# Sum stores and resident operand loads on other queues, and a bank read ahead of a tile's sums

## The chip, the cores and the metric

The kernel runs on one core of a Trainium2 chip. The metric is the device time of one execution in microseconds (us), as the median of several runs. The engines are TensorE (PE in the profile), VectorE (DVE), ScalarE (ACT), GpSimd (POOL) and SyncE (SP), which only issues transfers here. Each engine works through its own list of instructions in the written order, and they meet by semaphores.

## The reference

One layer of a decoder trunk on x of 2048 positions by 1024 features, all float32. The layer is a spatial-gating mixer, then a dense perceptron of four times the width with a squared ReLU, each behind an RMS norm and added to x, and a final RMS norm:

```python
def reference(x, ...):
    h = rmsnorm(x, norm_mix_g[0])
    x = x + mixer_chunked_sgu(h, a_w_in[0], a_v_g[0], a_w_s[0], a_b_s[0], a_w_out[0])
    x = x + channel_mlp(rmsnorm(x, norm_mlp_g[0]), mlp_w1[0], mlp_w2[0])
    return rmsnorm(x, final_g)

def channel_mlp(h, w1, w2):
    a = jax.nn.relu(h @ w1)
    return (a * a) @ w2
```

The mixer computes z = gelu(h @ w_in), splits it into u and v, mixes normed v within chunks of 128 positions by a causal matrix for each of 8 groups, and returns (u * s) @ w_out.

## The kernel before, in words

**Precision.** Every float32 operand is split into an upper part (a copy in fp32r, written by ScalarE, `_hi`) and a lower part (raw minus upper, written by VectorE, `_lo`). A product is three passes on TensorE: hi times hi, hi times lo, lo times hi (`PASSES`).

**Stages.** The mixer runs in 4 blocks of 512 positions (`block_pe`, `block_act`, `block_dve`). After the last block come 168 steps, numbered g. The perceptron is computed with a scheme of seven products of half-sized matrices in place of eight (`STEPS = 7`). Seven steps are a cycle. The up projection has 16 cycles u (`UP`), steps 0 to 111 (`SECOND` = 112), of 24 matmuls of 512 columns each; the down projection has 8 cycles, steps 112 to 167, of 48 matmuls each. Step 0 starts at 609.03 us, step 7 at 653.6 us, step 17 at 713.87 us, step 56 at 930.67 us and step 112 at about 1245 us of the span.

**Up projection.** For positions 0 to 1023 (cycles 0 to 7, the first pair) the seven operands `x_raw[0..6]` of 1024 KB stay resident; the second pair's replace them one by one around step 56. They come from the DRAM tensor `xs` (`up_operand`, line 319): those with `op < S2` are halves of the normed, transposed x1 (`x1T`), the others are sums of such, made by GpSimd. A weight `u_raw[g % 4]` of 512 KB is loaded for each step (`up_weight`, line 301), asked for when step g - 4 is done. ScalarE (`ahead`, `split_u`) and VectorE split the weight of step g + 2 at their step g, and then read the banks of step g: ScalarE those of steps 0, 2, 3 and 6 of a cycle (`keep_bank`, line 681), VectorE those of 1, 4 and 5 (`add_bank`, line 892). TensorE's step needs the split weight, the split operand, and that its banks have been read; the banks of step 3 of a cycle are those of step 1.

**Sums.** For each of two tiles j, ScalarE squares two of the four results into `sums[j][:, 0:2]` (`finish_first`, line 685, at step 6 of a cycle), and VectorE computes the rest with six instructions (`finish_second`, line 896), tile 0 at step 0 of the next cycle and tile 1 at its step 1, ahead of the bank read of that step. SyncE stores `sums[j]`, 1792 KB, to `a2s` (`keep_sums`, line 335) at steps 1 and 2 of the next cycle. ScalarE waits for the stores (`a2_stored`, line 689) before it writes the next cycle's; VectorE comes behind ScalarE by `first_half`.

**GpSimd's jobs.** `add_up` (line 438): load 1 MB to `job`, four instructions, store 1 MB; 40 in all, one buffer, so a job starts when the store before has landed. They make the sums of weights (`w1sum`, `w2sum`) and operands (`xs[:, 4:8]`). Twenty are done in the mixer; the loop at line 500 does two in each of cycles 0 and 1, one in each later cycle, and none in cycles 6 to 8. The first four of that loop are the second pair's operand sums; they wait until ScalarE's last `x1T` store has landed (line 453).

**Queues.** SyncE's list (line 350 on) issues in this order: the weights of the mixer; at the end of the last block operands 0 and 1 and the first four weights; behind the mixer's last product the operands 2 to 5; then the store of x1 to `x1s` (2 MB), and from step 0 on, at the end of each step, the next weight, operand 6 at step 1, the second pair's operands at steps 49 to 55, the sum stores, and for the down projection `down_operand` and `down_weight`. ScalarE's list has at the end of the last block the splits of operands 0 and 1 and of two weights, and then the squares of the four x1 tiles (line 642).

Of the kernel before, what the change touches and what calls it, by code (L numbers as in the profile page):

```python
# [30 lines left out]
def build(nc: bass.Bass, x, norm_mix_g, norm_mlp_g, final_g, a_w_in, a_v_g, a_w_s, a_b_s, a_w_out,  # L31
# [122 lines left out]
    with ExitStack() as ctx:  # L154
# [45 lines left out]
        a2_stored = [sem(f"a2_stored{s}") for s in range(2)]  # L200
# [77 lines left out]

        block = ctx.enter_context(nc.Block())

        @block.sync
        def _(sp):
# [36 lines left out]
            def up_operand(b, i):  # L319
                op = ACT_OPERAND[i]  # L320
                if op < S2:
                    sp.wait_ge(x1T_stored, 16 * 4 * (b + 1))
                else:
                    sp.wait_ge(job_stored, sums_stored("x", b))
                sp.dma_start(x_raw[i][:, :, :], xs[b][:, op, :].rearrange("p (k f) -> p k f", f=N))\
                    .then_inc(x_loaded[i], 16)

            def down_operand(d):
                n, i = d // STEPS, d % STEPS
                for s in range(2):  # L330
                    sp.wait_ge(a2_stored[s], 16 * 2 * (n + 1))
                sp.dma_start(a_raw[d % SLOTS][:, :, :], a2s[n][:, i, :].rearrange("p (k f) -> p k f", f=N))\
                    .then_inc(a_loaded[d % SLOTS], 16)

            def keep_sums(u, j):

                sp.wait_ge(second_half, 6 * (2 * u + j + 1))
                sp.wait_ge(first_half, 4 * (2 * u + j + 1))
                to = a2s[u // 2].rearrange("p i (k f) -> p i k f", f=N)[:, :, 2 * (u % 2) + j, :]
                sp.dma_start(to, sums[j][:, :, :]).then_inc(a2_stored[j], 16)  # L340
# [9 lines left out]
            for q in range(BLOCKS):  # L350
# [10 lines left out]
                else:  # L361

                    sp.wait_ge(mix_done, BLOCKS * G)
                    up_operand(0, 0)
# [3 lines left out]
                    up_operand(0, 1)  # L368
# [3 lines left out]
                    sp.wait_ge(products, done(number(q, 11)))  # L372
                    for i in range(2, 6):
                        up_operand(0, i)
                sp.wait_ge(x1_attn, (q + 1) * 2 * TT)
                sp.dma_start(x1s[q], x1[:, :, :]).then_inc(x1_stored, 16)
                if q < BLOCKS - 1:
                    sp.wait_ge(x1_stored, 16 * (q + 1))
                    sp.wait_ge(x1n_ready, (q + 1) * TT)
                    sp.dma_start(x1[:, :, :], x_v[q + 1]).then_inc(x1_loaded, 16)  # L380
            second = UP // PAIRS * STEPS
            for g in range(SECOND):
# [3 lines left out]
                if g == 1:  # L386
                    sp.wait_ge(x1_stored, 16 * BLOCKS)
                    sp.wait_ge(x1n_ready, BLOCKS * TT)
                    up_operand(0, 6)
                if second - STEPS <= g < second:  # L390
                    up_operand(1, g % STEPS)
                if g >= STEPS and g % STEPS in (1, 2):
                    keep_sums(g // STEPS - 1, g % STEPS - 1)
# [9 lines left out]
            for j in range(2):  # L403
                keep_sums(UP - 1, j)
            for d in range(SLOTS, DOWN * STEPS):
# [3 lines left out]
                if d == STEPS:  # L409
                    for h in range(2):  # L410
                        sp.wait_ge(a2_stored[h], 16 * UP)
# [8 lines left out]
        def _(pool):  # L420
# [78 lines left out]

            for u in range(UP):  # L500
                pool.wait_ge(products, step_done(u * STEPS))
                if not UP // PAIRS - 2 <= u <= UP // PAIRS:
                    next_jobs(2 if u < 2 else 1)
# [21 lines left out]
        def _(act):  # L525
# [74 lines left out]
            def block_act(q, last):  # L600
# [36 lines left out]
                else:  # L637
# [3 lines left out]
                    split_x(0, 1)  # L641
                for t in range(TT):
                    act.wait_ge(x1_attn, q * 2 * TT + TT + t + 1)
                    square(x1[:, t, :], x1_sq, t, x1_squares(q) + t)

# [39 lines left out]
            def finish_first(u, j):  # L685

                m = 2 * u + j
                if u:
                    act.wait_ge(a2_stored[j], 16 * u)
# [17 lines left out]
            for g in range(LAST):  # L707
                c, i = (g if g < SECOND else g - SECOND) // STEPS, g % STEPS
                ahead(g)
# [32 lines left out]
        def _(dve):  # L742
# [153 lines left out]
            def finish_second(u, j):  # L896
# [3 lines left out]
                a21 = r21[:, j, :]  # L900
                dve.wait_ge(act_read, banks_read(g + 6, j))
# [21 lines left out]
            for g in range(SECOND):  # L923
                c, i = g // STEPS, g % STEPS
                ahead(g)
                if c and i < 2:
                    finish_second(c - 1, i)
                if i in (1, 4, 5):
                    to = {1: c11, 4: c22, 5: c12}[i]
                    for j in range(2):  # L930
                        dve.wait_ge(act_read, banks_read({1: g - 1, 4: g - 1, 5: g - 3}[i], j))
                        add_bank(g, j, to[:, j, :])
                renew(g)
# [214 lines left out]
```

## Time and profile before

| | before |
|---|---|
| median of 3 runs | 1867.68 us (1865.74 to 1870.53) |
| profiled execution | 1867.12 us |
| its span | 1865.4 us |
| PE busy | 1827.3 us (98%) |
| DVE busy | 1052.2 us (56%) |
| ACT busy | 777.3 us (42%) |
| POOL busy | 401.2 us (22%) |
| DMA moved | 437.02 MB, 234 GB/s in the mean |
| SyncE's queue | 333.99 MB |
| GpSimd's queue | 92.80 MB |
| ScalarE's queue | 8.93 MB |
| granted TensorE clock | 0.993 |

Busy times are of the profiled execution, in us of its span. A row of waits names the engine and line that waited, what ended the wait, and the total, count and longest. A timeline row starts with start and duration; brackets show the idle time before it and its releaser.

### The profile page before, as it was taken

What the parts mean: (1) busy time and instruction counts of PE and PEld (TensorE: products, weight loads), DVE (VectorE), ACT (ScalarE), POOL (GpSimd) and SP (SyncE); (2) the same over time, 40 slices, a digit from 0 to 9 for tenths busy, and PEclk for the clock granted to TensorE, in tenths of its full rate; (3) what the DMA queues carried; (4) which work ended last, traced back from release to release, by engine and by line L of the source; (5) the groups of instructions that cost most, each with busy time, mean ns of one, the idle gap of its engine ahead of it and who ended that gap; (6) DMA issues with size and microseconds to landing.
All of it is one profiled execution on the core that took longest, in us unless ns stands there. A gap on an engine that the chain in (4) does not pass through costs nothing.

```text
span 1865.4 us, 20258 instructions
## 1 busy us (share of the span) xinstructions
PE 1827.3 (98%) x8329; PEld 1519.8 (81%) x8329; DVE 1052.2 (56%) x1009; ACT 777.3 (42%) x866; POOL 401.2 (22%) x390
## 2 busy tenths in 40 slices
PE   7999999999999998999989999999999999999998
PEld 6888888888888787888778888888888888888886
DVE  4464365265246656645565555557567666866665
ACT  5533544443442733344464433445333335333332
POOL 3341450351341033320001221110134202000001
PEclk9999999999999999999999999999999999999999
DMA  8545754762854787875856776699976754854552
GB/s 299 208 170 182 256 213 143 286 229 92 311 198 144 274 265 263 277 282 206 284 201 227 263 273 246 220 338 355 330 267 255 273 188 181 294 201 181 190 209 98
DMA packets 132092, 437.02 MB, mean 234 GB/s; under 512 B 7304, under 2 KB 8352, under 8 KB 117152
## 3 DMA queue, kind: packets, MB, share of 16 engines
q1 hardware_dynamic: 105488, 333.99, 50.4%
q0 software_dynamic: 25168, 92.80, 14.0%
q10 hardware_dynamic: 1344, 8.93, 1.2%
q8 instruction: 66, 1.08, 0.2%
q14 instruction: 26, 0.21, 0.0%
HBM read 309.87 MB, written 125.83 MB: 234 GB/s over the span
## 4 chain that ended last, share of the span: by engine, by line
PE 91%; DMA 3%; DVE 3%; ACT 1%; issue 1%; SPq 0%; POOL 0%; POOLq 0%; DVEq 0%; ACTq 0%
PE bank L1116 60%; PE bank L977 28%; PE bank L1014 2%; DMA u_raw<-in_mlp_w 1%; PE bank L1001 1%; DMA a_raw<-a2s 1%; DMA w_raw<-in_a_w_in 0%; DVE sums L912 0%; DVE u_lo L752 0%; DVE Y L919 0%; DVE r L902 0%; DVE sums L910 0%; DVE sums L908 0%; DVE sums L905 0%; ACT r L683 0%
## 5 line engine op out<-in xcount | busy, mean ns | idle before, releaser
L1116 PE MATMUL bank<-x_hi,u_hi 128*128 128x512 f32 x896 | 351.8, 393 | 16.1 <-DVE c L894 11.5
L1116 PE MATMUL bank<-x_lo,u_hi 128*128 128x512 f32 x896 | 350.7, 391 | 0.0
L1116 PE MATMUL bank<-x_hi,u_lo 128*128 128x512 f32 x896 | 350.6, 391 | 0.0
L1116 PE MATMUL bank<-d_hi,a_hi 128*128 128x512 f32 x896 | 348.8, 389 | 1.4 <-issue 1.0
L1116 PE MATMUL bank<-d_lo,a_hi 128*128 128x512 f32 x896 | 348.6, 389 | 0.0
L1116 PE MATMUL bank<-d_hi,a_lo 128*128 128x512 f32 x896 | 348.6, 389 | 0.0
L752 DVE TENSOR_TENSOR u_lo<-u_raw,u_hi 128x1024 fp32r<-128x1024 f32 x112 | 145.5, 1301 | 225.4 <-ACT u_hi L533 225.4
L894 DVE TENSOR_TENSOR Y<-bank,Y 128x512 f32<-128x512 f32 x208 | 137.8, 686 | 175.9 <-PE bank L1116 175.8
L746 DVE TENSOR_TENSOR w_lo<-w_raw,w_hi 128x2048 fp32r<-128x2048 f32 x48 | 119.4, 2494 | 187.5 <-ACT w_hi L528 187.5
L538 ACT ACTIVATE d_hi<-d_raw 128x2048 fp32r<-128x2048 f32 x56 | 107.4, 1919 | 279.8 <-DMA d_raw<-w2sum 150.9
L1116 PEld LDWEIGHTS bank<-x_hi,u_hi 128*128 128x128 f32 x896 | 169.6, 189 | 54.0 <-issue 15.7
L1116 PEld LDWEIGHTS bank<-x_hi,u_lo 128*128 128x128 f32 x896 | 169.5, 189 | 35.5
L1116 PEld LDWEIGHTS bank<-d_hi,a_hi 128*128 128x128 f32 x896 | 168.2, 188 | 37.1 <-issue 1.3
L1116 PEld LDWEIGHTS bank<-x_lo,u_hi 128*128 128x128 f32 x896 | 169.6, 189 | 35.1
L1116 PEld LDWEIGHTS bank<-d_lo,a_hi 128*128 128x128 f32 x896 | 168.2, 188 | 34.9
L1116 PEld LDWEIGHTS bank<-d_hi,a_lo 128*128 128x128 f32 x896 | 168.2, 188 | 34.9
L533 ACT ACTIVATE u_hi<-u_raw 128x1024 fp32r<-128x1024 f32 x112 | 118.4, 1057 | 171.5 <-DMA u_raw<-in_mlp_w 109.7
L769 DVE TENSOR_TENSOR a_lo<-a_raw,a_hi 128x2048 fp32r<-128x2048 f32 x56 | 132.4, 2364 | 20.2 <-ACT a_hi L547 20.1
L758 DVE TENSOR_TENSOR d_lo<-d_raw,d_hi 128x2048 fp32r<-128x2048 f32 x56 | 128.7, 2298 | 19.5 <-ACT d_hi L538 19.5
L547 ACT ACTIVATE a_hi<-a_raw 128x2048 fp32r<-128x2048 f32 x56 | 107.4, 1918 | 65.7 <-DMA a_raw<-a2s 65.7
L683 ACT ACTIVATE c<-bank 128x512 f32<-128x512 f32 x96 | 56.9, 597 | 164.8 <-PE bank L1116 164.7
L528 ACT ACTIVATE w_hi<-w_raw 128x2048 fp32r<-128x2048 f32 x48 | 91.5, 1913 | 33.6 <-DMA w_raw<-in_a_w_in 25.5
(107 smaller groups left out, 2739.6 us busy)
## 6 DMA issues: line engine op xcount, KB each, us to landing
a2s<-sums SPq DMA_DIRECT2D x32, 1792.0 KB, 10.7
a_raw<-a2s SPq DMA_DIRECT2D x56, 1024.0 KB, 7.5
w_raw<-in_a_w_in SPq DMA_DIRECT2D x32, 1024.0 KB, 5.9
job<-in_mlp_w POOLq DMA_DIRECT2D x32, 1024.0 KB, 7.0
u_raw<-w1sum SPq DMA_DIRECT2D x64, 512.0 KB, 4.4
d_raw<-w2sum SPq DMA_DIRECT2D x32, 1024.0 KB, 4.9
u_raw<-in_mlp_w SPq DMA_DIRECT2D x48, 512.0 KB, 5.5
d_raw<-in_mlp_w SPq DMA_DIRECT2D x24, 1024.0 KB, 5.2
```

The lines of the kernel that those rows point to most:

```text
L528: act.activation(w_hi[w % SLOTS][:, :, :], w_raw[w % SLOTS][:, :, :], ACT.Copy)\
L533: act.activation(u_hi[g % SLOTS][:, :, :], u_raw[g % SLOTS][:, :, :], ACT.Copy)\
L538: act.activation(d_hi[d % SLOTS][:, :, :], d_raw[d % SLOTS][:, :, :], ACT.Copy)\
L547: act.activation(a_hi[d % SLOTS][:, :, :], a_raw[d % SLOTS][:, :, :], ACT.Copy)\
L683: act.activation(to, bank_of(g, j)[:, :], func).then_inc(act_read, 1)
L746: dve.tensor_tensor(w_lo[s][:, :, :], w_raw[s][:, :, :], f32(w_hi[s][:, :, :]), ALU.subtract)\
L752: dve.tensor_tensor(u_lo[s][:, :, :], u_raw[s][:, :, :], f32(u_hi[s][:, :, :]), ALU.subtract)\
L758: dve.tensor_tensor(d_lo[s][:, :, :], d_raw[s][:, :, :], f32(d_hi[s][:, :, :]), ALU.subtract)\
L769: dve.tensor_tensor(a_lo[s][:, :, :], a_raw[s][:, :, :], f32(a_hi[s][:, :, :]), ALU.subtract)\
L894: dve.tensor_tensor(rows, bank_of(g, j)[:, :], rows, ALU.add).then_inc(dve_read, 1)
L977: ins = pe.matmul(BANK[s][j][:, :], stationary(x_part, k, j), moving(y_part, k, j), start=first and k == 0 and n == 0, stop=final and k == ...
L1116: ins = pe.matmul(bank_of(g, j)[:, :], stationary[x_part][:, k, j * P:(j + 1) * P], moving[y_part][:, k, :], start=i in (0, 1, 3) and k == ...
```

## The change

Three things move. The stores of the sums go from SyncE to GpSimd, each in two parts: operands 0 and 1 ahead of a cycle's first job, with a semaphore `a2_first`, and operands 2 to 6 behind it, with `a2_second`. ScalarE waits for the first part of the cycle before, and VectorE has a wait of its own for the second (`finish_second`). The loads of operands 2 to 5 of the first pair, of all seven of the second pair, and the last store of x1 go from SyncE to ScalarE. And at step 1 of a cycle VectorE reads its two banks ahead of tile 1's sums. The request for operand 6 of the first pair stands one step later.

```diff
@@ up_operand, now for a given engine @@
+        def up_operand(engine, b, i):
+            op = ACT_OPERAND[i]
+            if op < S2:
+                engine.wait_ge(x1T_stored, 16 * 4 * (b + 1))
+            else:
+                engine.wait_ge(job_stored, sums_stored("x", b))
+            engine.dma_start(x_raw[i][:, :, :], xs[b][:, op, :].rearrange("p (k f) -> p k f", f=N))\
+                .then_inc(x_loaded[i], 16)
@@ SyncE @@
             def down_operand(d):
                 n, i = d // STEPS, d % STEPS
                 for s in range(2):
-                    sp.wait_ge(a2_stored[s], 16 * 2 * (n + 1))
+                    sp.wait_ge(a2_first[s], 16 * 2 * (n + 1))
+                    sp.wait_ge(a2_second[s], 16 * 2 * (n + 1))
-            def keep_sums(u, j):
-
-                sp.wait_ge(second_half, 6 * (2 * u + j + 1))
-                sp.wait_ge(first_half, 4 * (2 * u + j + 1))
-                to = a2s[u // 2].rearrange("p i (k f) -> p i k f", f=N)[:, :, 2 * (u % 2) + j, :]
-                sp.dma_start(to, sums[j][:, :, :]).then_inc(a2_stored[j], 16)
-                    sp.wait_ge(products, done(number(q, 11)))
-                    for i in range(2, 6):
-                        up_operand(0, i)
-                sp.wait_ge(x1_attn, (q + 1) * 2 * TT)
-                sp.dma_start(x1s[q], x1[:, :, :]).then_inc(x1_stored, 16)
                 if q < BLOCKS - 1:
+                    sp.wait_ge(x1_attn, (q + 1) * 2 * TT)
+                    sp.dma_start(x1s[q], x1[:, :, :]).then_inc(x1_stored, 16)
-                if g == 1:
+                if g == 2:
                     sp.wait_ge(x1_stored, 16 * BLOCKS)
                     sp.wait_ge(x1n_ready, BLOCKS * TT)
-                    up_operand(0, 6)
-                if second - STEPS <= g < second:
-                    up_operand(1, g % STEPS)
-                if g >= STEPS and g % STEPS in (1, 2):
-                    keep_sums(g // STEPS - 1, g % STEPS - 1)
+                    up_operand(sp, 0, 6)
-            for j in range(2):
-                keep_sums(UP - 1, j)
@@ GpSimd @@
+            def keep_sums(u, part):
+
+                ops, count, of, kept = ((slice(0, 2), 4, first_half, a2_first),
+                                        (slice(2, STEPS), 6, second_half, a2_second))[part]
+                for j in range(2):
+                    pool.wait_ge(of, count * (2 * u + j + 1))
+                    to = a2s[u // 2].rearrange("p i (k f) -> p i k f", f=N)[:, ops, 2 * (u % 2) + j, :]
+                    pool.dma_start(to, sums[j][:, ops, :]).then_inc(kept[j], 16)
+
             for u in range(UP):
                 pool.wait_ge(products, step_done(u * STEPS))
-                if not UP // PAIRS - 2 <= u <= UP // PAIRS:
-                    next_jobs(2 if u < 2 else 1)
+                if u:
+                    keep_sums(u - 1, 0)
+                paused = UP // PAIRS - 2 <= u <= UP // PAIRS
+                if not paused:
+                    next_jobs(1)
+                if u:
+                    keep_sums(u - 1, 1)
+                if u < 2:
+                    next_jobs(1)
+            for part in range(2):
+                keep_sums(UP - 1, part)
@@ ScalarE, end of the last block @@
                     split_x(0, 1)
+                    act.wait_ge(products, done(number(q, 11)))
+                    up_operand(act, 0, 2)
+                    up_operand(act, 0, 3)
                 for t in range(TT):
                     act.wait_ge(x1_attn, q * 2 * TT + TT + t + 1)
                     square(x1[:, t, :], x1_sq, t, x1_squares(q) + t)
+                if last:
+                    act.dma_start(x1s[q], x1[:, :, :]).then_inc(x1_stored, 16)
+                    up_operand(act, 0, 4)
+                    up_operand(act, 0, 5)
@@ ScalarE, finish_first and the loop over steps @@
                 if u:
-                    act.wait_ge(a2_stored[j], 16 * u)
+                    act.wait_ge(a2_first[j], 16 * u)
+                if second - STEPS <= g - 1 < second:
+
+                    act.wait_ge(products, step_done(g - 1))
+                    up_operand(act, 1, (g - 1) % STEPS)
                 ahead(g)
@@ VectorE, finish_second and the loop over steps @@
+                if u:
+                    dve.wait_ge(a2_second[j], 16 * u)
                 dve.wait_ge(act_read, banks_read(g + 6, j))
-                if c and i < 2:
-                    finish_second(c - 1, i)
+                if c and i == 0:
+                    finish_second(c - 1, 0)
                 if i in (1, 4, 5):
                     to = {1: c11, 4: c22, 5: c12}[i]
                     for j in range(2):
                         dve.wait_ge(act_read, banks_read({1: g - 1, 4: g - 1, 5: g - 3}[i], j))
                         add_bank(g, j, to[:, j, :])
+                if c and i == 1:
+                    finish_second(c - 1, 1)
```

## Rows read from the trace of the kernel before

**Rows 1.** TensorE's waits: waiting line, what ended it; total us, count, longest.

```profile
PE bank L1116 <- DVE c L894: 11.5, 3, 6.0
PE bank L1116 <- issue: 3.6, 2, 2.6
PE bank L1116 <- DVE d_lo L758: 0.5, 1, 0.5
```

**Rows 2.** Timeline of TensorE: start, us, instruction, [idle before, releaser].

```profile
635.24 0.47 PE L1116 MATMUL bank<-x_hi,u_hi 128*128 128x512 f32 x1 [2.65 <-issue]
...
713.87 0.77 PE L1116 MATMUL bank<-x_hi,u_hi 128*128 128x512 f32 x1 [5.20 <-DVE c L894]
...
930.67 0.69 PE L1116 MATMUL bank<-x_hi,u_hi 128*128 128x512 f32 x1 [1.86 <-DVE u_lo L752]
...
955.31 0.76 PE L1116 MATMUL bank<-x_hi,u_hi 128*128 128x512 f32 x1 [6.02 <-DVE c L894]
```

**Rows 3.** Chain of waits in order of time: start, us, what.

```profile
635.24 5.73 PE bank L1116 x24
...
675.94 13.71 DMA u_raw<-in_mlp_w
...
713.87 204.08 PE bank L1116 x888
...
955.31 268.17 PE bank L1116 x1176
...
1268.74 582.37 PE bank L1116 x2568
```

**Rows 4.** Stretch 705 to 720: length, busy PE PEld DVE ACT POOL, clock, DMA, GB/s.

```profile
705.00:720.00 15.00, 9.80 (x33) 7.57 (x32) 11.51 (x12) 2.72 (x4) 5.68 (x5) 0.77 0.94 327
```

**Rows 5.** Timeline of SyncE's queue, issues with their time.

```profile
609.06 1.96 SPq L325 DMA_DIRECT2D x_raw<-xs  x4
...
664.94 0.60 SPq L340 DMA_DIRECT2D a2s<-sums  x1
```

**Rows 6.** Timeline of ScalarE around the first steps; the next instruction is at 639.24.

```profile
607.75 1.06 ACT L566 ACTIVATE junk<-x 128x1024 bf16<-128x1024 f32 x1 [21.23 <-DVE x L813]
...
615.00 1.91 ACT L543 ACTIVATE x_hi<-x_raw 128x2048 fp32r<-128x2048 f32 x1
...
638.87 0.33 ACTq L597 DMA_DIRECT2D xs<-x1T  x1
```

**Rows 7.** Timeline of VectorE: an operand's lower half, bank reads, a tile's sums.

```profile
616.94 2.29 DVE L763 TENSOR_TENSOR x_lo<-x_raw,x_hi 128x2048 fp32r<-128x2048 f32 x1 [2.10 <-ACT x_hi L543]
...
713.03 1.28 DVE L894 TENSOR_TENSOR c<-bank,c 128x512 f32<-128x512 f32 x2
...
740.03 1.23 DVE L752 TENSOR_TENSOR u_lo<-u_raw,u_hi 128x1024 fp32r<-128x1024 f32 x1 [5.12 <-ACT u_hi L533]
741.17 0.69 DVE L902 TENSOR_TENSOR r<-r 128x512 f32<-128x512 f32 x1
...
744.42 0.69 DVE L914 TENSOR_TENSOR sums<-sums 128x512 f32<-128x512 f32 x1
```

**Rows 8.** Timeline of GpSimd: a job's load and store, the next job's instructions and store.

```profile
649.79 0.83 POOL L454 DMA_DIRECT2D job<-xs  x1 [36.26 <-DMA xs<-x1T]
...
664.19 0.78 POOL L475 DMA_DIRECT2D xs<-job  x1 [0.30 <-POOL job L473]
...
684.41 1.29 POOL L467 TENSOR_TENSOR job<-job 128x512 f32<-128x512 f32 x1 [11.92 <-DMA job<-xs]
...
690.10 0.78 POOL L475 DMA_DIRECT2D xs<-job  x1 [0.30 <-POOL job L473]
```

**Rows 9.** 600 to 720: landings of job transfers, of sum stores; job load of 718.8.

```profile
DMA to landing us min/median/max: 5.3/7.3/12.6
...
DMA to landing us min/median/max: 8.6/12.4/17.3
...
job<-xs POOLq DMA_DIRECT2D x1, 1024.0 KB, 8.3
```

More of the change, by code:

```diff
@@ L199, in build @@
         first_half, second_half = sem("first_half"), sem("second_half")
-        a2_stored = [sem(f"a2_stored{s}") for s in range(2)]
+        a2_first = [sem(f"a2_first{s}") for s in range(2)]
+        a2_second = [sem(f"a2_second{s}") for s in range(2)]
         x1_added = [sem(f"x1_added{i}") for i in range(4)]
@@ L317, in down_weight @@
                 sp.dma_start(d_raw[d % SLOTS][:, :, :], src).then_inc(d_loaded[d % SLOTS], 16)
[L319 to L326, printed above, removed]
             def down_operand(d):
@@ L363, in _ @@
                     sp.wait_ge(mix_done, BLOCKS * G)
-                    up_operand(0, 0)
+                    up_operand(sp, 0, 0)
                     sp.wait_ge(products, done(number(q, 8)))
@@ L367, in _ @@
                     up_weight(1)
-                    up_operand(0, 1)
+                    up_operand(sp, 0, 1)
                     sp.wait_ge(products, done(number(q, 9)))
@@ L380, in _ @@
                     sp.dma_start(x1[:, :, :], x_v[q + 1]).then_inc(x1_loaded, 16)
-            second = UP // PAIRS * STEPS
             for g in range(SECOND):
@@ L410, in _ @@
                     for h in range(2):
-                        sp.wait_ge(a2_stored[h], 16 * UP)
+                        sp.wait_ge(a2_first[h], 16 * UP)
+                        sp.wait_ge(a2_second[h], 16 * UP)
                         sp.dma_start(Y[1][h][:, :, :], x1s[2 + h]).then_inc(Y_loaded[h], 16)
@@ L708, in _ @@
                 c, i = (g if g < SECOND else g - SECOND) // STEPS, g % STEPS
+                second = UP // PAIRS * STEPS
+                if second - STEPS <= g - 1 < second:
+                    act.wait_ge(products, step_done(g - 1))
+                    up_operand(act, 1, (g - 1) % STEPS)
                 ahead(g)
```

## The prediction

> **What bounds the kernel now.** I began with the busy shares of the page: TensorE is busy in 98% of the span, so the whole question is which of its few pauses go and which come. The list of waits gives them by what ended them [rows 1], the timeline of TensorE gives their place [rows 2], and the chain of waits gives the length of the stretches between them [rows 3]. Up to 609 us nothing that the change touches stands near a pause. From there to the end six pauses matter. Steps are numbered as in the loops, step g being one operand product of the multilayer perceptron. An undisturbed step of the up projection is 24 matmuls; the last long stretch, 2568 matmuls in 582.37 us [rows 3], makes that 5.44 us.
> The pauses are 2.65 us before step 4, 5.20 before step 17, 1.86 before step 56 and 6.02 before step 59 [rows 2]. The vector engine's reads of a bank stand behind 11.5 us in three pauses [rows 1]; less the two long ones that leaves 0.28 us, before step 10. The two small ones at the start of the down projection are 0.5 us and what the second "issue" wait leaves, 3.6 - 2.65 = 0.95 [rows 1]. After a pause TensorE runs slowly for a while: the stretch of 705 to 720 us was granted 0.77 of the clock [rows 4], between its levels of 1.2 and 2.4 GHz. Priced against 226.8 ns a matmul, the stretch from 713.87 lost 2.7 us and that from 955.31 lost 1.5; the three steps between 930.67 and 949.29 (955.31 less its pause) took 18.62 us where 16.33 were due, 2.3 lost; step 4 took 5.73, 0.3 lost [rows 2, 3]. Together: 2.95 (step 4) + 0.28 + 7.90 (step 17) + 4.15 (step 56) + 7.50 (step 59) + 1.45 = 24.2 us. That is the most this change can win. The profiled execution took 1867.12 us around a span of 1865.4; without the six pauses it would be 1842.9. The median of the runs is 0.56 above the profiled one.
> Why they are there: a store of the sums (1792 KB) is issued on SyncE's queue between weight loads, as at 664.94 [rows 5], and the chain shows a weight load issued at 675.94 that landed 13.71 us later [rows 3]. ScalarE and VectorE take everything in a written order, so a late weight makes all behind it late, and VectorE's 3.9 us of sums for the second tile then stand in front of its bank read.
>
> **The change part by part.**
> *Bank reads first.* At the second step of a cycle VectorE now reads the two banks before the second tile's six sums. Nothing is added. The reads took from 713.03 and TensorE went on at 713.87 [rows 2, 7]; at 3.9 us earlier, the 0.28 goes and most of 5.20 and 6.02 would, if all else stood still. What is late next is the weight split of the step after, which still comes behind the sums.
> *Sum stores to GpSimd's queue.* This takes the stores out of the way of the weight loads. Around step 56 the loads of the second pair's seven operands leave SyncE's queue too, for ScalarE's, each behind a wait for a step that ScalarE was about to wait for anyway. Walking ScalarE's list from step 50, weights landing in the median of some 5 us, I find step 56 served about 4 us ahead and step 59 about 2 us ahead; so 1.86 + 2.3 + 6.02 + 1.5 go, as does the 1.45 at the end, whose operand load was behind a sum store. Seven issues of 0.37 us (638.87 to the next ScalarE instruction [rows 6]) lie in ScalarE's idle time. Cover gone, this costs at most what stands there now.
> *The start of the up projection.* ScalarE now waits for the end of the mixer's last product, where SyncE issued at 609.06 [rows 5], then issues two loads, squares four tiles, and issues the store of x1 and two more loads. Before, the first square began at 607.75 [rows 6]. The wait and two issues (0.4 each) make the squares 2.1 us later, three issues more make 3.3. The split of operand 2 then moves from 615.00 [rows 6] to 618.3, its lower half from 616.94 [rows 7] to 620.2 and its end to 622.5. Step 2 is due at 619.9 (609.03 and two steps), so TensorE pauses 2.6 us there, 0.3 with the clock. In exchange weight 4 no longer stands behind 6 MB, and the pause before step 4 goes. Issues at SyncE's 0.49 each (1.96 for four [rows 5]) instead of 0.37 move this by 0.6; the bounds are 2.0 and 4.0, and I take 2.9. Operand 6 is asked for one step later on SyncE, but the x1 store that it waits for is what held it, and it has a whole step in hand: nothing.
> *The new place of the stores, and the new wait.* This is the costly part. GpSimd also does the "jobs" (load 1 MB, four tensor instructions, store 1 MB, the next only after that store landed). In cycles 0 and 1 it does two jobs each. The second part of the sums of cycle u-1 (five of seven operands) is issued behind the first job of cycle u, and VectorE may not write the sums of cycle u before it has landed. What waits behind VectorE is the weight split of the step after next, and behind that TensorE.
> The job that starts at 649.79 [rows 8] cannot start sooner, for it waits for the last x1T store. It stores at 664.19, which alone on the queues takes the least of the job transfers, 5.3 us [rows 9]: 669.5. The next load is given 6.3, between least and median 7.3; instructions to store 5.7 (684.41 to 690.10 [rows 8]): 681.5. Only now GpSimd comes to cycle 1. The first part of the sums is issued behind that store and lands some 9 us later, in time, as ScalarE wants it at about 690. Next job: store landed 687.8 (6.3), load 8.3 as in the row with a store beside it [rows 9], 5.7 more: 701.8. Behind it come the two second parts, 1280 KB each. The least landing of 1792 KB is 8.6 and of 1024 KB is 5.3 [rows 9], so 4.3 us per 1000 KB; the queue's 2304 KB up to the first tile make 10.8: 712.6. VectorE's sums for one tile take 3.9 (741.17 to 745.11), a split 1.15, the bank read and TensorE's start 0.8 [rows 7]: step 17 can start at 718.4. It would have been due at 713.87 - 5.20 - 0.28 - 0.3 = 708.1. **A new pause of 10.3 us** and 2.7 of slow clock.
> Cycle 2, the same way: the stores of cycle 1 end at 701.8 + 16.3 = 718.1; the fourth job's load is behind them, 722.5; its store 728.2; landed 734.5; next load 742.8; store 748.5; first tile's second part 759.3; step 24 at 765.1. It is due at 718.4 + 38.1 + 2.7 = 759.2: **a pause of 5.9** and 2.3 slow. In cycle 3 there is one job only, the stores land about 783 to 790 while VectorE comes to them at about 790: no pause. Later the second part lands some 27 us after the first step of a cycle, and VectorE comes 36 us after it.
> Bounds for the two pauses with their clock, 21.2 us: every job transfer at its least and the stores at 8.6 give about 15; 4 us more on the chain give about 25.
> The sum: 1842.9 + 2.9 + 13.0 + 8.2 = 1867.0, plus 0.56 for the median, **1867.6**: no change, because the pauses removed around 714, 931 and 955 us are paid for at steps 2, 17 and 24.
>
> **A page against it.** At 705 to 720 us the DMA engines were busy in 0.94 of the time at 327 GB/s [rows 4]. The Trainium skill (DMA: Bandwidth & Descriptors, Issuing engines are not separate DMA queues) says that transfers from whichever issuer share the same 16 engines, and that another issuer saves issue time only. By that rule the weight load at step 52 stays late and the pause before step 56 stays. The row of 13.71 us [rows 3] doesn't settle it: a full set of engines and a store ahead in the queue look alike there.
> The first VectorE sum at 741.17 runs beside no GpSimd instruction; GpSimd's issue at 649.79 took 0.83 and that at 664.19 took 0.78 with VectorE at work [rows 8]. The Trainium skill (SBUF — State Buffer, Who interferes with whom) warns that a DMA from GpSimd can be starved of descriptors by VectorE. These rows show no such thing, and the rule would put the result with the slow rival below.
>
> **The rivals.**
> (a) *Exchange*, the forecast: 1861 to 1875 by the bounds above.
> (b) *GpSimd keeps up*: VectorE's new wait never ends last. For it: GpSimd is busy in only 22% of the span. Against it: the serial chain from 649.79, each link a row. The time is 1842.9 + 2.9 + 0.56 = 1846.4; with one short pause left, 1855.
> (c) *Slower*: in cycles 1 and 2 the transfers go at the saturated ends of the rows, loads at 12.6 and sum stores at 17.3 [rows 9], since weights, jobs and sums now all run at once. Two loads (6.3 and 4.3 more) and the stores (3 to 5 more) put step 17 some 15 us later, and cycle 2 follows by 3 more: 1867.6 + 18 = 1885. The place is VectorE's wait at steps 14 and 21. It turns the result slower by over 0.3% once the two pauses pass some 22 us together, where I have 16.2.
> (d) *Queues make no difference*: shared engines keep the weights as late as they are, and the 1.86 + 2.3 at step 56 stay: 1867.6 + 4.2 = 1871.8. For it speaks the DMA share of 0.94 [rows 4]; against it, that a weight load alone needs half a megabyte in each step and gets a turn of its own.
>
> **How the numbers follow.** About 0.3%, 5.6 us, is what a measurement of this kernel can tell from no change (its three runs lie 4.8 apart). Chances: (a) 0.56, of which 0.11 under 1862, 0.39 within, 0.06 over 1873; (b) 0.26, all faster; (c) 0.14, all slower; (d) 0.04, within. So faster 0.37, same 0.43, slower 0.20. The range of 0.8 takes in (b) down to 1847 and goes up to 1878, into the lower part of (c). The forecast's own range is 1861 to 1875.
>
> **What would show it.** In the new profile: TensorE's waits by VectorE's bank reads at step 10 and 59 gone, the wait before step 4 gone and one of 2 to 4 us before step 2 (about 620 us); a VectorE gap before its first sum at about 698 to 712 us ended by a sum store, and TensorE pauses at about 708 (step 17) and 759 (step 24), 10 and 6 us; none from 800 us to the end of the up projection. If the gap on VectorE is there but ends before 702 us, (b) holds. If the weight loads around 912 us still take over 12 us to land, (d) holds. The forecast is wrong above all if GpSimd issues the second part of cycle 0 much sooner or later than 702 us.

## The result, and the profile after

The changed kernel takes 1874.1 us in the median (1873.0 to 1876.2), the kernel before, run beside it, 1869.3. The ratio of the means is 1.0031, with a 95% interval of 1.0018 to 1.0044: 5 us slower by the medians, 6 by the means. The forecast was 1867.6, no change. The profiled execution took 1874.05 us around a span of 1872.3, against 1867.12 before, so the two traces can be compared directly. Two single executions of kernels below stand far outside, at 2221.8 us (operand loads back on SyncE) and 4786.0 us (old queues); the ratios leave them out.

The page after: TensorE is still the bound, and the bytes have changed queues (rows of section 1 and 3; SyncE's queue is q1, GpSimd's q0, ScalarE's q10).

```profile
span 1872.3 us, 20356 instructions
...
PE 1827.2 (98%) x8329; PEld 1520.2 (81%) x8329; DVE 1057.5 (56%) x1009; ACT 775.1 (41%) x866; POOL 448.3 (24%) x454
...
q1 hardware_dynamic: 74576, 261.64, 38.9%
q0 software_dynamic: 40528, 151.53, 23.1%
q10 hardware_dynamic: 3072, 22.56, 3.0%
```

TensorE works as long as before, to 0.1 us. The difference is in its pauses. TensorE's timeline after, every idle time ahead of a product of the perceptron:

```profile
622.51 0.47 PE L1136 MATMUL bank<-x_hi,u_hi 128*128 128x512 f32 x1 [1.47 <-issue]
...
723.03 0.76 PE L1136 MATMUL bank<-x_hi,u_hi 128*128 128x512 f32 x1 [15.09 <-DVE c L910]
...
732.74 0.50 PE L1136 MATMUL bank<-x_hi,u_hi 128*128 128x512 f32 x1 [1.53 <-DVE u_lo L768]
...
768.79 0.47 PE L1136 MATMUL bank<-x_hi,u_hi 128*128 128x512 f32 x1 [3.12 <-DVE c L910]
...
963.27 0.47 PE L1136 MATMUL bank<-x_hi,u_hi 128*128 128x512 f32 x1 [2.16 <-DVE c L910]
...
970.97 0.50 PE L1136 MATMUL bank<-x_hi,u_hi 128*128 128x512 f32 x1 [0.40 <-DVE u_lo L768]
```

These stand before steps 2, 17, 18, 24, 59 and 60. Set against [rows 2], the pauses before steps 4 and 56 are gone, that before step 17 has grown from 5.20 to 15.09, and that before step 59 has shrunk from 6.02 to 2.16. Priced as in the prediction (5.44 us for an undisturbed step), the stretches behind the pauses took 0.3, 2.7, 0.3, 1.8 and, for the last two together, 1.9 us more than was due. The clock granted behind the pauses of steps 17, 24 and 59 was 0.68, 0.85 and 0.76 (723.1 to 731.2, 768.8 to 780 and 963.4 to 970.4 us); behind those of steps 2 and 18 it was 1.00, so the two 0.3 are not the clock's. The list is 23.8 us of pauses and 6.9 of slower work behind them, 30.7; the time without them is 1843.3, where the prediction has 1842.9. Before, the same account gave 24.2 (24.8 with two stretches of 0.3 that the prediction left out). That is 5.9 of the 6.9 us between the two executions. The rest, some 1.1, lies ahead of the first step: step 0 begins at 610.16 us and not at 609.03. In the kernels below it begins between 609.08 and 610.37, with the old queues as late as with the new; I count it to the run and not to the change.

How the long pause comes about is in the chain of waits (start, duration, what), here from 664 to 734 us:

```profile
664.74 6.25 DMA xs<-job
671.28 7.28 DMA job<-xs
...
690.97 9.80 DMA job<-xs
...
707.34 9.83 DMA a2s<-sums
...
732.74 22.07 PE bank L1136 x96
```

and in the timeline, GpSimd's rows and VectorE's:

```profile
685.96 1.43 POOL L493 DMA_DIRECT2D a2s<-sums  x2
690.97 0.75 POOL L440 DMA_DIRECT2D job<-xs  x1 [3.58 <-DMA xs<-job]
...
706.57 0.78 POOL L461 DMA_DIRECT2D xs<-job  x1 [0.30 <-POOL job L459]
707.34 1.74 POOL L493 DMA_DIRECT2D a2s<-sums  x2
...
717.19 0.69 DVE L920 TENSOR_TENSOR r<-r 128x512 f32<-128x512 f32 x1 [16.19 <-DMA a2s<-sums]
...
722.20 1.28 DVE L910 TENSOR_TENSOR c<-bank,c 128x512 f32<-128x512 f32 x2
...
725.68 1.76 DVE L926 TENSOR_TENSOR sums<-sums,r 128x512 f32<-128x512 f32 x1
```

GpSimd issues the first parts of cycle 0's sums at 685.96, behind two jobs, and the second parts at 707.34, behind a third. VectorE's first sum of cycle 1 waits 16.19 us for that store, its bank read follows at 722.20, and TensorE starts step 17 at 723.03.

### The profile page after: what moved, and what is told of

Same layout as the page of the kernel before. It is cut to its first block, busy times and chain, and to the rows that moved or that the text cites. A ratio compares the mean times of both kernels' runs of the same rounds, so it can differ in the third digit from the quotient of the medians.

```text
span 1872.3 us, 20356 instructions
## 1 busy us (share of the span) xinstructions
PE 1827.2 (98%) x8329; PEld 1520.2 (81%) x8329; DVE 1057.5 (56%) x1009; ACT 775.1 (41%) x866; POOL 448.3 (24%) x454
## 4 chain that ended last, share of the span: by engine, by line
PE 90%; DMA 4%; DVE 2%; ACT 1%; POOL 1%; issue 1%; SPq 0%; POOLq 0%; ACTq 0%; DVEq 0%
PE bank L1136 59%; PE bank L997 28%; PE bank L1034 2%; DMA job<-xs 1%; PE bank L1021 1%; DMA xs<-job 1%; DMA u_raw<-w1sum 1%; DMA u_raw<-in_mlp_w 1%; DMA a2s<-sums 1%; DMA w_raw<-in_a_w_in 0%; DVE u_lo L768 0%; ACT x_hi L547 0%; POOL job L459 0%; DVE Y L937 0%; ACT x1T L597 0%
## 5 line engine op out<-in xcount | busy, mean ns | idle before, releaser
L1136 PE MATMUL bank<-x_hi,u_hi 128*128 128x512 f32 x896 | 351.7, 392 | 23.8 <-DVE c L910 20.4
L493 POOL DMA_DIRECT2D a2s<-sums x64 | 51.2, 806 | 287.7 <-PE bank L1136 217.0
```

Source lines behind the costliest of these rows:

```text
L493: pool.dma_start(to, sums[j][:, ops, :]).then_inc(kept[j], 16)
L1136: ins = pe.matmul(bank_of(g, j)[:, :], stationary[x_part][:, k, j * P:(j + 1) * P], moving[y_part][:, k, :], start=i in (0, 1, 3) and k == ...
```

## Experiments

The theory: the pauses at steps 17, 18 and 24 come from GpSimd's list, in which the sum stores stand behind jobs that each wait for their own transfers. Cycles 0 and 1 have two jobs each, so cycles 1 and 2 begin with the list behind. The rivals: full DMA engines, or the stores' length, make VectorE wait wherever the stores are issued; or another part of the change costs the time. Unless told otherwise an edit is made to the changed kernel, and ratios are to the kernel before. All but the last two ran on one chip, the last two on another, each beside the kernel before, whose median was 1867.5 to 1868.2 us.

### The second parts ahead of the job

```diff
                 if u:
                     keep_sums(u - 1, 0)
+                    keep_sums(u - 1, 1)
                 ...
                     next_jobs(1)
-                if u:
-                    keep_sums(u - 1, 1)
```

> The changed kernel, but GpSimd issues both parts of a cycle's sum stores before the cycle's job, not around it. My theory (the serial list of GpSimd: VectorE's new wait ends late in cycles 1 and 2 only because two jobs and a job's load stand in front of the second part): the pauses before steps 17, 18 and 24 (15.09 + 1.53 + 3.12 us) and their slow clock (4.8) go, so about 1849.5 us, 1846 to 1855; pauses before steps 2 and 59 stay as they are. Rival (shared engines: the bytes of jobs, sums and weights are what takes the time, in whatever order they are issued): the second part still lands at 710 or later, step 17 still pauses 8 us or more, 1866 or more.

Measured: 1864.0 us, 0.9978 (0.9969 to 0.9987), between the two and nearer to the rival's number, 10 us under the changed kernel. No pause stands before step 17, but beside the one before step 2 there are five, of 1.2 to 5.6 us, at steps 18, 23, 25, 59 and 60. The timeline of this kernel, rows of GpSimd, ScalarE and TensorE:

```profile
685.36 3.16 POOL L493 DMA_DIRECT2D a2s<-sums  x4
690.53 0.75 POOL L440 DMA_DIRECT2D job<-xs  x1 [2.00 <-DMA xs<-job]
708.68 1.56 POOL L453 TENSOR_TENSOR job<-job 128x512 f32<-128x512 f32 x1 [17.40 <-DMA job<-xs]
...
741.99 0.63 ACT L703 ACTIVATE c<-c 128x512 f32<-128x512 f32 x1 [15.21 <-DMA a2s<-sums]
...
749.48 0.79 PE L1135 MATMUL bank<-x_hi,u_hi 128*128 128x512 f32 x1 [5.62 <-DVE u_lo L767]
```

The wait moved. The third job's load now follows 3.5 MB of sum stores in GpSimd's queue and its first instruction starts 18.15 us after its issue, where the median of the job transfers before was 7.3 [rows 9]; everything behind it in the list is later, and it is now the first part of cycle 1's sums that comes late, with ScalarE waiting 15.21 us for it. While the list is too long, the order in it decides who waits and for how long; it doesn't end the waiting. My expectation took the jobs to be free to slip; they are not.

### One job a cycle from the start

```diff
-                if u < 2:
-                    next_jobs(1)
```

> The changed kernel, but with one job instead of two in cycles 0 and 1; the three jobs fewer end up in later cycles and in the down projection. Theory (serial list): GpSimd is free at about 671 us, the second part of cycle 0 goes out at about 687 and lands before 702, so steps 17 and 24 do not pause: 1849 to 1854, less good than with the second part first only if the later jobs hold the down projection. Rival (a job's load between the two parts is enough to make the second late): step 17 still pauses over 5 us, 1862 or more.

Measured: 1867.4 us, 0.9996 (0.9988 to 1.0005). By its number this is the rival's, by its places it is not. The up projection came out as the theory says: TensorE runs without a pause from 641.85 us for 1176 matmuls, through steps 17, 18 and 24. What I had named as a proviso and given no price is the far end: the last jobs are stored later, at 1474.63 us, and SyncE's loads of the down projection, in one list, wait for the sum of weights that they make (the chain of this kernel, then TensorE's timeline):

```profile
641.85 266.59 PE bank L1134 x1176
...
1442.92 7.13 DMA job<-in_mlp_w
...
1474.63 4.57 DMA w2sum<-job
...
1479.76 8.71 DMA a_raw<-a2s
```

```profile
1493.47 0.76 PE L1134 MATMUL bank<-d_hi,a_hi 128*128 128x512 f32 x1 [12.59 <-DVE Y L908]
```

The loads behind that store cost one pause of 12.59 us. So the doubled jobs have a purpose, but not their place. That asked for a kernel that keeps all forty and moves two.

### The two doubled jobs moved to cycles 11 and 13

```diff
-                if u < 2:
+                if u in (11, 13):
                     next_jobs(1)
```

> The changed kernel with one job instead of two in cycles 0 and 1, and two instead of one in cycles 11 and 13, so that as many jobs as before are done by the down projection. With one job a cycle the up projection had pauses of 1.5, 2.1 and 2.0 us only, and the down projection one of 12.6 for a late job. Theory (serial list of GpSimd): that one goes too and a second job in a later cycle has its 38 us: 1867.4 - 12.6 - 1.25 - 2.5 of slow clock = 1851, 1848 to 1855. Rival (the second job makes its own pause in cycles 12 and 14): 1858 or more.

Measured: 1856.2 us, 0.9939 (0.9927 to 0.9950). It is 1 us outside the range of 1848 to 1855 and under the rival's 1858. Against the changed kernel's 1.0031 that is 0.0092, 17 us, from two jobs put elsewhere, and nothing stands before steps 17, 18 and 24. This settles the theory: same stores, same queues, same bytes, and the pauses go with the place of the jobs. Most of the 5 us that it lacks of the 1851 lies in one pause at the start of the down projection (the timeline of GpSimd and TensorE):

```profile
1217.19 2.79 POOL L445 TENSOR_TENSOR job<-job 128x512 f32<-128x512 f32 x1 [17.57 <-DMA job<-in_mlp_w]
...
1258.05 0.76 PE L1136 MATMUL bank<-d_hi,a_hi 128*128 128x512 f32 x1 [6.49 <-DVE a_lo L785]
```

The job of cycle 15 waits 17.57 us for its load. The second part of cycle 14's sums is issued behind it and lands at 1249.57; VectorE's sums of cycle 15 wait for that, and the splits of the down projection's operands stand behind those sums.

### The sum stores back on SyncE

```diff
@@ SyncE, each tile in one piece @@
+                if g >= STEPS and g % STEPS in (1, 2):
+                    keep_sums(g // STEPS - 1, g % STEPS - 1)
 ...
@@ GpSimd @@
-                    keep_sums(u - 1, 0)
 ...
-                    keep_sums(u - 1, 1)
@@ VectorE @@
-                if u:
-                    dve.wait_ge(a2_second[j], 16 * u)
```

with GpSimd's loop as it was before (two jobs in cycles 0 and 1). Bank reads and operand loads stay as changed.

> The changed kernel with the sum stores back on SyncE in one piece, without VectorE's wait for the second part; operand loads on ScalarE and early reads stay. Theory: no pause at steps 17 and 24; the start pauses 1.5 instead of 2.3 and 1.6 of slow clock; around steps 56 to 60 the sum stores still stand ahead of the weights, but no operand does, so about half of the 7.5 us of pauses there stay: 1853, 1850 to 1857. Rival (shared engines: whose queue the operand loads are on changes nothing): 1857 to 1859, as with the early reads alone.

Measured: 1859.7 us, 0.9958 (0.9945 to 0.9971). The 16.19 us wait of VectorE is gone and with it the long pause, which puts the loss on the stores' place a second time, from the other side. It is not as fast as I expected: it lies outside the range of 1850 to 1857 and a shade over the rival's 1857 to 1859, that is, level with the early reads alone (0.9946, below). The pause before step 56 is back. TensorE's timeline:

```profile
926.79 0.80 PE L1124 MATMUL bank<-x_hi,u_hi 128*128 128x512 f32 x1 [3.90 <-DVE u_lo L758]
```

The weight loads go with it. The longest one near step 56, here (issued between 905 and 910 us) and in the changed kernel (at 933.87), by issuer, size in KB and us to landing:

```profile
u_raw<-in_mlp_w SPq DMA_DIRECT2D x1, 512.0 KB, 19.2
...
u_raw<-in_mlp_w SPq DMA_DIRECT2D x1, 512.0 KB, 10.0
```

### The bank reads, undone and alone

Undone in the changed kernel; the second edit is its reverse, made to the kernel before:

```diff
-                if c and i == 0:
-                    finish_second(c - 1, 0)
+                if c and i < 2:
+                    finish_second(c - 1, i)
                 ...
-                if c and i == 1:
-                    finish_second(c - 1, 1)
```

> The changed kernel with VectorE's old order: at step 1 of a cycle the second tile's sums ahead of the bank reads. Theory: the early reads are worth 4 to 8 us at step 17 (the sums of the second tile took 8.1 us there beside GpSimd's instructions), about 4 at step 59, and under 4 at step 24: 1874.1 + 10 = 1884, 1879 to 1889. Rival (the reads are not what ends last, a weight or the other tile is): within 2 us of 1874.

Measured: 1883.8 us, 1.0081 (1.0065 to 1.0097), as expected, and 9.7 us over the changed kernel. TensorE's timeline:

```profile
729.85 0.77 PE L1134 MATMUL bank<-x_hi,u_hi 128*128 128x512 f32 x1 [22.41 <-DVE c L910]
...
969.97 0.76 PE L1134 MATMUL bank<-x_hi,u_hi 128*128 128x512 f32 x1 [6.03 <-DVE c L910]
```

The sums of the second tile are in front of the bank read again: step 17 pauses 22.41 us, and step 59 6.03, as in [rows 2].

> The kernel before with only VectorE's new order (bank reads ahead of the second tile's sums). Theory: the 0.28 us before step 10 goes, the 5.20 before step 17 shrinks to some 1.2 with half of its slow clock, and of the 6.02 before step 59 only 1.4 go, since the weight split of the step after is then late behind the sums: 1869.3 - 7 = 1862, 1859 to 1866. Rival (the pause only moves one step on): 1867 to 1870.

Measured: 1857.8 us, 0.9946 (0.9933 to 0.9958): 9.8 us faster than before, with all transfers where they were, and better than the 1859 to 1866 expected. No pause is left before step 17, where I had kept 1.2 us. In place of the two before steps 56 and 59 there are four, of 1.6 to 2.2 us, at steps 56, 58, 59 and 60. So this part alone is worth 10 us, in either surrounding, and the changed kernel would be faster than before had it been the only change.

### The operand loads back on SyncE

```diff
@@ SyncE @@
+                    sp.wait_ge(products, done(number(q, 11)))
+                    for i in range(2, 6):
+                        up_operand(sp, 0, i)
+                if second - STEPS <= g < second:
+                    up_operand(sp, 1, g % STEPS)
@@ ScalarE @@
-                    up_operand(act, 0, 2)
 ...
-                    up_operand(act, 1, (g - 1) % STEPS)
```

and so for the x1 store and operand 6; the sum stores stay with GpSimd.

> The changed kernel with the operand loads and the last x1 store back on SyncE; sum stores on GpSimd and early reads stay. Theory (the sum stores' new place alone makes the slowdown): the pauses of 15 and 3 us at steps 17 and 24 stay, the pause at step 2 becomes one of 2.6 before step 4, and around step 59 weights stand behind operands: 1876, 1873 to 1879. Rival (ScalarE's extra issues and waits cost something that the list of pauses hides): below 1872.

Measured: 1875.0 us, 1.0033 (1.0017 to 1.0048), level with the changed kernel. Its profiled execution was 8.6 us shorter than its median, so its pauses can't be summed to that; only their places are read: step 2's pause is gone, and the one before step 4 is back at 2.40 us. The operand loads' queue is worth nothing that can be measured.

### Around step 56

All kernels so far have pauses at steps 56 to 60, where the second pair's operands are loaded and split. In all of them ScalarE and VectorE split one operand in each of seven successive steps, 52 to 58. The edit, made to the kernel of cycles 11 and 13, in both engines' lists, spreads these splits by when each operand is needed:

```diff
                 elif second - 4 <= g < second - 4 + STEPS:
-                    split_x(1, g - second + 4)
+                    for i in {-4: (0,), -3: (1,), -2: (2, 3), 0: (4,), 2: (5,)}.get(g - second, ()):
+                        split_x(1, i)
+                elif g == second + 3:
+                    split_x(1, 6)
```

> As the one with the jobs moved later, and the second pair's operands are split at other steps, on ScalarE and VectorE: operands 2 and 3 both at step 54, 4 at 56, none at 57, 5 at 58, 6 at 59. Theory (at steps 55 to 57 ScalarE and VectorE have more to do than two steps hold, after a weight that came 10 us late): the pauses of 2.1 and 2.0 us before steps 59 and 60 and 1.9 us of slow clock go: 5 to 6 us less than that kernel, about 1846. Rival (the late weight load alone makes them, since the engines are full there): within 1.5 us of it.

Measured: 1849.7 us, 0.9908 (0.9895 to 0.9920), 6.5 us less. The up projection has no pause at all behind step 2, though the weights issued at 898 to 909 us still took 9.2 to 9.8 us to land, with all DMA engines busy (a share of 1.00 from 906 to 923 us). Part of the gain may be the 6.49 us pause at 1258, which in this kernel's profile is 1.81; the pauses at 930 to 946 were 4.5 us with no clock counted.

### The jobs off the last cycle

The edit is made to the kernel of the last section.

```diff
-                if not paused:
+                if not paused and u < UP - 1:
                     next_jobs(1)
                 ...
-                if u in (11, 13):
+                if u in (4, 10, 12):
                     next_jobs(1)
```

> As the one with the moved operand splits, but the doubled jobs are in cycles 4, 10 and 12, and cycle 15 has none, so that nothing stands between the two parts of the sum stores where the down projection's loads begin. Theory: with a job in cycle 15 its load took 15 to 18 us there, the second part landed late and TensorE paused 1.8 us (6.5 in the kernel without the moved splits) before step 113; that goes: 2 to 4 us less than 1849.7, about 1847, with a pause near 1.9 us at the start as the only one. Rival (the loads of the down projection make that pause themselves): 1849 to 1851.

Measured: 1846.5 us, 0.9881 (0.9868 to 0.9895), the fastest here: 22 us under the kernel before and 28 under the changed one. Its timeline of GpSimd and VectorE up to cycle 1, and TensorE's waits in the perceptron (line, what ended them; total, count, longest):

```profile
664.52 1.43 POOL L493 DMA_DIRECT2D a2s<-sums  x2
...
685.31 1.74 POOL L493 DMA_DIRECT2D a2s<-sums  x2
...
695.22 0.69 DVE L926 TENSOR_TENSOR r<-r 128x512 f32<-128x512 f32 x1 [1.56 <-DMA a2s<-sums]
```

```profile
PE bank L1142 <- issue: 1.5, 1, 1.5
PE bank L1142 <- DVE c L916: 1.3, 2, 1.0
```

First and second parts go out 21.4 and 22.0 us earlier than in the changed kernel, with one job less ahead of each. VectorE still waits for the store, 1.56 us in place of 16.19, and TensorE does not notice.

### The same edits with the old queues

Is the stores' move worth anything once the rest is mended? This kernel is the one before with VectorE's new order and the spread splits, all transfers as before.

> The kernel before with the early reads and the moved operand splits, all transfers where they were. Theory (the splits' place and not the queues makes the pauses before steps 59 and 60): these two, 2.2 and 2.0 us, and their slow clock go and the ones before steps 56 and 58 (1.6 and 1.7, a weight behind a sum store) stay: 1857.8 - 5 = 1853, 1851 to 1856. Rival (with the weights late behind stores, ScalarE is late anyway and the splits' order changes nothing): 1857 to 1859.

Measured: 1854.4 us, 0.9917 (0.9902 to 0.9932). The kernel with the moved transfers and placed jobs is 0.0036 below that, some 7 us, on the same chip. How the 7 us divide over stores, operand loads and jobs was not measured. What the traces do show is the stores' effect around step 56. In the four kernels with the sum stores on SyncE (before, early reads alone, stores back on SyncE, and this one) the longest weight landing there is 15.5 to 19.2 us, and TensorE pauses 1.6 to 3.9 us before step 56. In the eight with the stores on GpSimd it is 8.8 to 10.9 us, and none pauses there. So the stores out of the weights' way remove that pause; their share of the 7 us stays open.

## Why the prediction was wrong

The exchange was right as a mechanism, and so were the places of the pauses at steps 2, 17 and 24. The two after step 56 were forecast as gone, and the one at step 18 not at all. The sum was 6.6 us short of the profile (24.1 forecast, 30.7 found): step 17 +4.8, step 18 +1.8, steps 59 and 60 +4.4, less 3.3 at step 24 and 1.2 at the start. So two things failed: the links of GpSimd's chain up to step 17 were sized too short, and step 59 was put at nothing. That the time still lies inside the forecast's 1861 to 1875 is in part luck, by the two terms that erred the other way. Term by term:

**What the pauses cost before, and the floor.** 1842.9 forecast, 1843.3 found. Right. (The prediction speaks of six pauses and sums seven.)

**Start pause, step 2.** 2.9 forecast, 1.7 found (1.47 and 0.3). TensorE started at 622.51, which is the 622.5 forecast, but by two errors that cancel: step 0 began 1.1 us later than the prediction reckoned, and the way from there was 1.1 us shorter. The three issues priced as a delay lay beneath the last square (timeline of ScalarE):

```profile
614.83 1.06 ACT L570 ACTIVATE junk<-x 128x1024 bf16<-128x1024 f32 x1
614.87 0.33 ACTq L653 DMA_DIRECT2D x1s<-x  x1
```

In the six kernels below with the same start that begin step 0 at 609.1 to 609.7 us the pause is 1.5 to 2.0 us too, so the 2.6 was an overlap left out and not the mixer's doing. The pause before step 4 went, as forecast.

**Step 17.** 13.0 forecast, 17.8 found (15.09 and 2.7). Due at 708.1, found 723.03 - 15.09 = 707.94. From GpSimd's issue of the second parts to VectorE's first sum 10.8 forecast, 717.19 - 706.57 = 10.6 found from the store ahead; from there to TensorE 5.8, found 5.84. The clock 2.7, found 2.7. What failed is the chain in between, in which I took values at or under the median for three of four transfers. The first job began 1.6 us later than the 649.79 of [rows 8] (651.35, and 1.1 of it is the mixer). Its store came only 0.55 late, at 664.74. From there to the next load were 6.5 us (forecast 5.3), on to the store 13.9 (12.0: the load took 7.28 to land, not 6.3, and the instructions with the gap ahead of the store 6.5, not 5.7), to the load after that 5.8 (6.3), and to its store 15.6 (14.0; the load 9.80, not 8.3). That is 0.55 + 1.2 + 1.9 - 0.5 + 1.6 = 4.8 us at the last job's store (706.57 against 701.8), and the pause is 4.8 longer than forecast (15.1 against 10.3). Four of five links missed on the same side, by 0.6 to 1.9 us each. The first parts of the sums, forecast to land in time, did not: ScalarE waited 8.28 us for them, until 693.56, which TensorE did not notice.

**Step 18.** Nothing forecast, 1.8 found. The second tile's sums ran from 723.39 to 731.5, 8.1 us where I had priced 3.9, and the weight split behind them was late. I had said of VectorE's sums only that one of them ran beside no GpSimd instruction before; that the new wait puts them beside a job's instructions was there to see. The trace before has their price too (timeline of VectorE; at 744.42 the same instruction took 0.69 [rows 7]):

```profile
704.28 1.66 DVE L914 TENSOR_TENSOR sums<-sums 128x512 f32<-128x512 f32 x1
```

**Step 24.** 8.2 forecast, 4.9 found (3.12 and 1.8). The pauses at 17 and 18 pushed its due time to 765.67, forecast 759.2, while the chain came out 3.7 late (768.79 against 765.1). An error upstream was given back in part.

**Steps 56 to 60.** "4 us ahead" at step 56: no pause, right. "2 us ahead" at step 59: wrong, 4.4 us found (2.16, 0.40 and 1.9 of clock). The premise that failed is "weights landing in the median of some 5 us". A link of the chain, and the window of 930 to 947 us (length, busy of PE, PEld, DVE, ACT and POOL, clock, DMA share, GB/s), show why:

```profile
933.87 9.99 DMA u_raw<-in_mlp_w
```

```profile
930.00:947.00 17.00, 17.00 (x76) 14.08 (x76) 12.76 (x10) 10.17 (x11) 0.00 (x0) 1.00 1.01 413
```

A weight with nothing but weights in SyncE's queue took 9.99 us with all DMA engines busy; those issued from 917 to 934 us took 9.1 to 10.0. The late weight is half of the cause only. With the splits spread the weights landed as late (9.2 to 9.8 us) and no pause was left, so what held step 59 is a late weight together with seven operand splits in successive steps of ScalarE's and VectorE's lists, which the walk along ScalarE's list had not priced.

To this extent rival (d) held, but not by its own sign (over 12 us for the weights around 912 us; the one there took 6.4), and not at step 56, where no pause is left. The rule of the Trainium skill that the prediction quoted for it (DMA: Bandwidth & Descriptors, Issuing engines are not separate DMA queues) has two parts. That transfers share the 16 engines whoever issues them: the trace agrees, by the 9.99 us and by the run with the operand loads back on SyncE, 0.9 us from the changed kernel. That another issuer saves issue time only: here the runs differ, for with the sum stores back in SyncE's queue a weight took 19.2 us where the changed kernel's longest took 10.0.

**The rivals.** (b), GpSimd keeps up, is refuted by the 16.19 us wait. (c) named the right side and the point from which it turns slower, pauses of over some 22 us at steps 17 and 24; with step 18 they came to 19.7, and the 4.4 at steps 59 and 60, which (c) had not counted, took the kernel to the 0.3%. But its price was too high: ahead of step 17 the loads took 7.3 and 9.8 us, not 12.6, and the second parts' stores 9.8 and some 13, not 17.3. Only the next load, at 711.90, came near, with 11.9. The two pauses with their clock came to 22.7, in the upper part of the 15 to 25 that I had bounded them by.

**Balance of the parts.** Three runs lead from the kernel before to the changed one, a part at a time: bank reads alone 0.9946; with the operand loads on ScalarE 0.9958; with the sum stores in GpSimd's list 1.0031. In us, -10, +2 and +14; the +2 is within the intervals of the two ratios (0.9933 to 0.9958 and 0.9945 to 0.9971) and can't be told from nothing. That the gains and the cost about cancel was in the forecast; what it lacked is the size of the cost.

## What to carry to other kernels

Before moving a transfer to an engine that is little busy, read that engine's list and not its share: GpSimd was busy in 24% of the span, and still the second parts went out 21 us after the first, behind one job that waits for landings of its own. If a serial list becomes the path, put its links at the loaded rows of the trace, since the errors add up, and ask what in the list can go elsewhere: here two jobs moved by some ten cycles were worth 17 us. Measure the parts of a change alone: the one that moved no transfer was worth 10 us, hidden by the loss of another.

## What the runs showed of the hardware

**VectorE beside GpSimd.** The same sum instruction, 128x512 with two inputs from SBUF, took 0.68 us at 718.41 and 1.76 us at 725.68, the latter beside GpSimd's job instructions (timeline after):

```profile
718.41 0.68 DVE L926 TENSOR_TENSOR sums<-sums,r 128x512 f32<-128x512 f32 x1
...
725.28 1.61 POOL L455 TENSOR_TENSOR job<-job 128x512 f32<-128x512 f32 x1
726.97 1.60 POOL L457 TENSOR_TENSOR job<-job 128x512 f32<-128x512 f32 x1
```

GpSimd's own took 1.60 to 1.62 here and 1.28 to 1.31 at 700 us, where VectorE mostly stood still. From start to start each engine did one instruction in 1.7 us here, where alone VectorE needs 0.60 and GpSimd 1.36: nearly the sum. The Trainium skill (SBUF — State Buffer, Who interferes with whom) says that the two engines share a pair of SBUF ports behind an exclusive lock; the trace agrees in so far as they go nearly one after the other. That the lock is held for a whole instruction is not shown.

**GpSimd's DMA issues** were not held up by VectorE: the pair at 731.34 took 1.44 us, 0.72 each, with VectorE starting on three weight splits, and the mean of all 64 is 0.81. No starving of GpSimd's issues, which the prediction had weighed, shows in them.

**A load behind stores.** In GpSimd's queue a 1 MB load took 6.44 and 7.28 us with nothing of GpSimd's ahead (651.35, 671.28), 9.80 behind the first parts of the sums (1 MB, 690.97), 11.9 behind the second parts (2.5 MB, 711.90), and some 18 behind 3.5 MB of them. The DMA engines were busy in 0.80 and 0.77 of the time of the first two, and in 0.96, 0.91 and 0.95 of the others, so queue and engines can't be told apart by these rows.
